# The first recurrent columns multiplied inside the modulation stage of a one-core diffusion block

## What is computed

```python
m_lat = split(silu(c) @ w_mod + b_mod, 6)            # shift, scale, gate, ... for x
m_ctx = split(silu(c_ctx) @ w_mod + b_mod, 6)        # the same for ctx
hx = rmsnorm(x, norm_mix) * (1 + m_lat[1]) + m_lat[0]
hc = rmsnorm(ctx, norm_mix) * (1 + m_ctx[1]) + m_ctx[0]
qx, kx, vx, lx, lgx, bgx, cgx, ux, gx = split_cols(hx @ w_in)   # and of hc
lru = scans(gates(conv(lx)), from ctx) * gelu(lgx)   # recurrent branch, both directions
```

## Time and profile before

| | us |
|---|---|
| median of 3 runs | 2921.41 (2920.41 to 2923.23) |
| the profiled execution, its time | 2924.9 |
| its span | 2922.7 |
| PE busy in the span | 2596.3 (89%) |
| DVE busy | 1912.2 (65%) |
| ACT busy | 947.9 (32%) |
| mean granted PE clock | 0.977 |

### The profile page before, as it was taken

How to read it: one execution, slowest core, us unless ns; L and a number is a source line. 1 busy time by engine, 2 the same in 40 slices (tenths; PEclk the granted TensorE clock), 3 DMA queues, 4 the chain that set the end, 5 groups by cost and what they waited for, 6 DMA issues and landing times.

```text
span 2922.7 us, 30747 instructions
## 1 busy us (share of the span) xinstructions
PE 2596.3 (89%) x11077; PEld 1764.0 (60%) x11077; DVE 1912.2 (65%) x2614; ACT 947.9 (32%) x1303; POOL 560.2 (19%) x580
## 2 busy tenths in 40 slices
PE   5899999999999999999999997777878877777777
PEld 3578877888777899998887843232434323332332
DVE  2589997434777778887556865666555665556656
ACT  3477875433554333333444211111101111111110
POOL 0000000000000000000000653433333333333333
PEclk7899999999999999999999999999999999999999
DMA  8733335543327788886575999999999999999998
GB/s 353 295 115 119 116 110 195 190 157 115 130 87 297 299 320 335 337 338 258 202 273 220 396 421 422 421 421 422 421 421 421 421 421 421 421 422 421 421 421 345
DMA packets 126356, 901.77 MB, mean 309 GB/s; under 512 B 14000, under 2 KB 15536, under 8 KB 17200
## 3 DMA queue, kind: packets, MB, share of 16 engines
q0 software_dynamic: 82944, 604.02, 50.1%
q1 hardware_dynamic: 38448, 276.84, 25.1%
q10 hardware_dynamic: 4864, 19.61, 1.7%
HBM read 898.29 MB, written 2.13 MB: 308 GB/s over the span
## 4 chain that ended last, share of the span: by engine, by line
PE 53%; DMA 36%; DVE 5%; issue 4%; ACT 1%; POOL 0%; POOLq 0%; ACTq 0%; DVEq 0%
DMA u<-in_peer_u,idx 31%; PE ps L473 12%; PE ps L516 8%; PE ps L518 8%; PE ps L517 8%; PE ps L488 6%; DVE u L1994 3%; DMA v<-in_peer_v,idx 2%; PE ps L870 2%; DMA w<-in_stream 2%; PE ps L582 2%; PE ps L893 1%; PE ps L699 1%; PE ps L682 1%; PE ps L531 1%
## 5 line engine op out<-in xcount | busy, mean ns | idle before, releaser
L893 PE MATMUL ps<-v,dg 128*128 128x512 f32 x1920 | 901.4, 618 | 246.2 <-DMA v<-in_peer_v,idx 205.2
L1994 DVE SCALAR_TENSOR_TENSOR u<-u,hN 128x2048 f32<-128x2048 f32 x256 | 586.5, 2291 | 461.0 <-DMA u<-in_peer_u,idx 460.8
L893 PEld LDWEIGHTS ps<-v,dg 128*128 128x128 f32 x1920 | 359.7, 195 | 782.2 <-issue 437.1
L1356 DVE TENSOR_TENSOR wl<-w,wh 128x1024 fp32r<-128x1024 f32 x428 | 519.8, 1222 | 360.4 <-ACT wh L992 359.8
L992 ACT ACTIVATE wh<-w 128x1024 fp32r<-128x1024 f32 x428 | 450.9, 1059 | 606.3 <-PE ps L518 400.2
L2100 POOL DMA_INDIRECT u<-in_peer_u,idx x256 | 260.8, 1019 | 930.9 <-DVE u L1994 546.8
L473 PE MATMUL ps<-both,wh 128*128 128x256 f32 x2048 | 371.8, 284 | 0.0
L1296 ACT ACTIVATE dg<-con,wt 128x128 f32<-128x128 f32 x240 | 92.7, 399 | 807.5 <-PE ps L893 802.5
L473 PEld LDWEIGHTS ps<-both,wh 128*128 128x128 f32 x2048 | 320.1, 192 | 3.5 <-issue 3.3
L473 PE MATMUL ps<-both,wl 128*128 128x256 f32 x1024 | 289.8, 283 | 0.0
L2084 POOL DMA_DIRECT2D mr<-in_wmod x64 | 34.0, 532 | 1306.0 <-DVE br_lo L1743 893.3
(11 more groups left out here) (287 smaller groups left out, 2737.1 us busy)
## 6 DMA issues: line engine op xcount, KB each, us to landing
w<-in_stream SPq DMA_DIRECT2D x258, 1024.0 KB, 4.9
mr<-in_wmod POOLq DMA_DIRECT2D x64, 1024.0 KB, 7.1
wg<-in_gates ACTq DMA_DIRECT2D x8, 512.0 KB, 3.4
wx<-in_stream SPq DMA_DIRECT2D x4, 1024.0 KB, 9.2
u<-in_peer_u,idx POOLq DMA_INDIRECT x256, 16.8
v<-in_peer_v,idx POOLq DMA_INDIRECT x256, 18.0
xs<-in_ctx ACTq DMA_DIRECT2D x1, 2048.0 KB, 16.4
xs<-in_x ACTq DMA_DIRECT2D x1, 2048.0 KB, 25.7
```

The costliest lines, as they stand in the source:

```text
L893: last = mm(ps[:, b, :], dg[:, k % 4, :], V[n % NV][:, b * 512:(b + 1) * 512], start=(k == 0), stop=(k == TOPK - 1))
L1356: tt(wl[p % SPLITS][:, :, :], W[s][:, q * PIECE:(q + 1) * PIECE, :], wh[p % SPLITS][:, :, :].bitcast(F32), ALU.subtract)\
L1994: stt(U[n % NU][:, :], U[n % NU][:, :], 1.0, hN[t][:, :], ALU.mult, ALU.mult, accum_out=dot[:, t, k:k + 1])\
```

## The change

- SP issues the loads of `par`, `ctx` and `x` ahead of the first halves; ACT issues only `con`. ACT waits for `par` alone, DVE for `con` before `sel`. Squares and scaling of the tokens follow at once.
- The transposes move into turn 1 of the modulation, four k-tiles behind each half (`x_turned`), over three banks (5 to 7) instead of four.
- The two halves of the first 256 columns of `lx` go to buffers `E[0]`, `E[1]` of their own (where `xs` lay), loaded among the halves after turns 2 and 3; slots 0 and 1 aren't loaded again for them.
- `early(k)`: two plain fp32 products of 128x512, weights of `E` stationary, the modulated k-tile of `xT` (both sides) moving, into banks 6 and 7. 13 of the 16 calls stand behind halves of turns 3 to 7 (`EARLY_AT`), number 13 ahead of the last `rows_turn`, 14 and 15 behind it. `first_piece` is gone, with its four splits and four lows; `hi_done` and `lo_done` are raised by four instead.
- `pads(0)` reads banks 6 and 7. Lows 4 and 5 come directly behind the last `tile_lows`, then the memset of `pad`, which waits for the last early product, then the load of `wg`, split 6, the pads and split 7.
- `mod_rows` and `mod_cols` follow the turns one by one; the exception for turn 2 is gone.

```diff
+        E = [sb(f"e{i}", R_BR + i * HB, [P, HK, CW]) for i in (0, 1)]
...
+        EARLY_AT = {(3, 0): (0,), (3, 1): (1,), (3, 2): (2,), (3, 3): (3,), (4, 0): (4,), (4, 1): (5,), (4, 3): (6,),
+                    (5, 0): (7,), (5, 3): (8,), (6, 0): (9,), (6, 3): (10,), (7, 0): (11,), (7, 3): (12,)}
+        EARLY_BANK = 6
...
+            sp.dma_start(par[:, :], a_params).then_inc(par_in, 16)
+            sp.dma_start(xs[:, 0:2, :], a_ctx.rearrange("(t p) d -> p t d", p=P)).then_inc(xc_in, 16)
+            sp.dma_start(xs[:, 2:4, :], a_x.rearrange("(t p) d -> p t d", p=P)).then_inc(xs_in, 16)
...
+                    if i == MODS and s < 2:
+                        sp.sem_inc(arrived[s], 16)
+                        continue
                     sp.dma_start(W[s][:, :, :], a_stream[i * RING + s].rearrange("p (k n) -> p k n", n=CW)).then_inc(arrived[s], 16)
+                if i in (2, 3):
+                    sp.wait_ge(*P0.at(0, f"xT{KT - 1}"))
+                    sp.dma_start(E[i - 2][:, :, :], a_stream[LRU0 + i - 2].rearrange("p (k n) -> p k n", n=CW)).then_inc(e_in[i - 2], 16)
...
-                    if n == 1 and c and c != 3:
+                    if n == 1 and c:
                         rows_turn(c - 1)
+                    if c == 1:
+                        x_turned(4 * n)
+                    for k in EARLY_AT.get((c, n), ()):
+                        early(k)
...
+            def x_turned(k0):
+
+                if k0 == 0:
                     pe.wait_ge(*A0.at(0, "xn1"))
                     pe.wait_ge(*V0_.at(0, "xn3"))
...
+                for k in range(k0, k0 + 4):
+                    if k >= 3:
+                        pe.wait_ge(xt_copied[(k - 3) % 2], (k - 3) // 2 + 1)
+                    for t in range(4):
+                        last = nc.tensor.transpose(ps[:, 5 + k % 3, t * P:(t + 1) * P], xs[:, t, k * P:(k + 1) * P], ident)
+                    last.then_inc(*P0.inc(f"xT{k}"))
+
+            def early(k):
+
+                pe.wait_ge(e_in[k // HK], 16)
+                pe.wait_ge(*VV.at(k, "x"))
+                pe.wait_ge(*AH.at(k, "vc"))
+                for blk in (0, 1):
+                    last = mm(ps[:, EARLY_BANK + blk, :], E[k // HK][:, k % HK, blk * P:(blk + 1) * P], xT[:, k, :],
+                              start=(k == 0), stop=(k == KT - 1))
+                if k == KT - 1:
+                    last.then_inc(piece_used, 4)
+
+            pe.wait_ge(*V0_.at(0, "st"))
+            for c in range(MODS):
                 mod_turn(c)
+            early(KT - 3)
             rows_turn(MODS - 1)
-            for p in range(4):
-                first_piece(p)
+            early(KT - 2)
+            early(KT - 1)
...
-            pads(0, 2 * LRU0 + 4)
+            pads(0, 2 * LRU0 + 4, EARLY_BANK)
...
             tile_lows(MODS - 2)
             tile_lows(MODS - 1)
-            low(LRU0, 0, 0, 2)
-            low(LRU0, 0, 0, 3)
+            dve.sem_inc(lo_done, SPLITS)
+            low(LRU0, 0, 0, 4)
+            low(LRU0, 0, 0, 5)
             dve.wait_ge(*VH.at(KT - 1, "lo_x"))
+            dve.wait_ge(piece_used, 2 * LRU0 + 4)
             nc.vector.memset(pad[:, :, :, :], 0.0).then_inc(*VZ.inc("lru"))
```

More of the change, by code:

```diff
@@ L296, in build @@
         apart_count = [sem("apart_dve"), sem("apart_pool")]
-        par_in, xs_in = sem("par_in"), sem("xs_in")
+        par_in, con_in, xc_in, xs_in = sem("par_in"), sem("con_in"), sem("xc_in"), sem("xs_in")
+        e_in = [sem(f"e_in{i}") for i in (0, 1)]
         wg_in, x2_in, m_in = sem("wg_in"), sem("x2_in"), sem("m_in")
@@ L945, in _ @@
             fn = nc.scalar.activation
-            act.dma_start(par[:, :], a_params).then_inc(par_in, 16)
-            act.dma_start(con[:, :], a_consts).then_inc(par_in, 16)
-            act.wait_ge(par_in, 32)
+            act.dma_start(con[:, :], a_consts).then_inc(con_in, 16)
+            act.wait_ge(par_in, 16)
             fn(sig0[:, :], pc("c", 0, 2 * KT), ACT.Sigmoid).then_inc(*A0.inc("sig"))
@@ L964, in _ @@
             fn(lm[2][:, :], lm[1][:, :], ACT.Exp, scale=-1.0).then_inc(*A0.inc("ez"))
[L965 to L968, removed]
             for i in range(4):
+                act.wait_ge((xc_in, xs_in)[i // 2], 16)
                 if i:
@@ L980, in _ @@
                 act.wait_ge(*P0.at(0, f"xT{k}"))
-                fn(xT[:, k, :], ps[:, 4 + k % 4, :], ACT.Copy).then_inc(xt_copied[1], 1)
+                fn(xT[:, k, :], ps[:, 5 + k % 3, :], ACT.Copy).then_inc(xt_copied[1], 1)
             def split(first, turn, per, p, slots=None):
@@ L989, in split, with pads @@
                     return
-                if first != LRU0 or p >= SPLITS:
+                if first != LRU0 or p >= 2 * SPLITS:
                     act.wait_ge(piece_used, turn * per + (2 * first + p - SPLITS + 1))
                 fn(wh[p % SPLITS][:, :, :], W[s][:, q * PIECE:(q + 1) * PIECE, :], ACT.Copy).then_inc(hi_done, 1)
-            for c in range(MODS - 1):
+            for c in range(MODS):
                 tiles(c)
[L997 to L1001, removed]
+            act.sem_inc(hi_done, SPLITS)
+            split(LRU0, 0, 0, AHEAD - 1)
+            split(LRU0, 0, 0, 5)
             act.wait_ge(*VZ.at(0, "lru"))
             act.dma_start(wg[:, :, :, :], a_gates[0].rearrange("p (b g n) -> p b g n", b=2, g=4)).then_inc(wg_in, 16)
-            split(LRU0, 0, 0, AHEAD - 1)
-            split(LRU0, 0, 0, 5)
             split(LRU0, 0, 0, 6)
-            def pads(j, used):
+            def pads(j, used, bank=0):
                 act.wait_ge(piece_used, used)
@@ L1013, in pads @@
                     act.wait_ge(*VT.at(j - 1, f"tap{b}3"))
-                    fn(pad[:, b, :, LRU_TAPS // 2:LRU_TAPS // 2 + T], ps[:, b, :].rearrange("p (s t) -> p s t", s=2), ACT.Copy)\
+                    fn(pad[:, b, :, LRU_TAPS // 2:LRU_TAPS // 2 + T], ps[:, bank + b, :].rearrange("p (s t) -> p s t", s=2), ACT.Copy)\
                         .then_inc(*AD.inc(f"pad{b}"))
-            pads(0, 2 * LRU0 + 4)
+            pads(0, 2 * LRU0 + 4, EARLY_BANK)
             split(LRU0, 0, 0, 7)
@@ L1346, in _ @@
             tt(sQ[:, :, 0:2], by_k(sig0[:, :]), by_k(pc("c", 0, 2 * KT)), ALU.mult).then_inc(*V0_.inc("st"))
+            dve.wait_ge(con_in, 16)
             nc.vector.reduce_sum(sel[:, :], ident.rearrange("p (g v) -> p v g", v=QUAD), AX.X).then_inc(*V0_.inc("sel"))
@@ L1416, in _ @@
             tsc(cof[:, 1, :], lm[5][:, :], -8.0, None, ALU.mult).then_inc(*V0_.inc("c8"))
-            for c in range(2):
-                mod_rows(c)
-                mod_cols(c)
             dve.wait_ge(*A0.at(0, "rt"))
@@ L1424, in _ @@
                 tsc(xs[:, i, :], xs[:, i, :], rin0[:, i:i + 1], None, ALU.mult).then_inc(*V0_.inc(f"xn{i}"))
-            mod_rows(2)
-            mod_rows(3)
+            mod_rows(0)
             for k in range(0, KT, 2):
                 dve.wait_ge(*P0.at(0, f"xT{k}"))
-                nc.vector.tensor_copy(xT[:, k, :], ps[:, 4 + k % 4, :]).then_inc(xt_copied[0], 1)
+                nc.vector.tensor_copy(xT[:, k, :], ps[:, 5 + k % 3, :]).then_inc(xt_copied[0], 1)
+                if k == 2:
+                    mod_cols(0)
             dve.wait_ge(xt_copied[1], KT // 2)
             dve.wait_ge(xt_copied[0], KT // 2)
[L1432 to L1441, removed]
+            values_x(0)
+            mod_rows(1)
+            for c in range(1, MODS - 1):
                 mod_cols(c)
@@ L1445, in _ @@
                 mod_rows(c + 1)
-            tile_lows(MODS - 2)
             mod_cols(MODS - 1)
             values_x(MODS - 1)
-            low(LRU0, 0, 0, 0)
-            low(LRU0, 0, 0, 1)
+            tile_lows(MODS - 2)
             tile_lows(MODS - 1)
-            low(LRU0, 0, 0, 2)
-            low(LRU0, 0, 0, 3)
+            dve.sem_inc(lo_done, SPLITS)
+            low(LRU0, 0, 0, 4)
+            low(LRU0, 0, 0, 5)
             dve.wait_ge(*VH.at(KT - 1, "lo_x"))
+            dve.wait_ge(piece_used, 2 * LRU0 + 4)
             nc.vector.memset(pad[:, :, :, :], 0.0).then_inc(*VZ.inc("lru"))
@@ L1556, in lru_turn @@
                 lru_out(j, 1)
-            low(LRU0, 0, 0, 4)
-            low(LRU0, 0, 0, 5)
             low(LRU0, 0, 0, 6)
@@ L1615, in _ @@
             dve.wait_ge(gains_in, 32)
-            dve.wait_ge(par_in, 32)
+            dve.wait_ge(con_in, 16)
             turned = lambda x: x.rearrange("p t (a s j) -> p t a s j", a=2, s=2)
```

## The result

| | before | after |
|---|---|---|
| median, us (6 runs each) | 2923.25 | 2903.06 |
| range | 2920.41 to 2926.05 | 2900.1 to 2905.19 |
| the profiled execution: time, span | 2924.9, 2922.7 | 2905.19, 2903.1 |
| mean granted PE clock | 0.977 | 0.988 |

The ratio is 0.9934 with a 95% interval of 0.9923 to 0.9944: 0.66% faster by the ratio, 20.2 us by the medians. Forecast was 22.5 us, from 2921.4 to 2899; the runs lie between 2900 and 2905, inside 2893 to 2910.

The account below looks back on a forecast made before the run. HBM was taken to bound the kernel until about 108 us, then PE. A clean gain of 25.4 us, less 3 us for the clock, gave 22.5 with rounding: 2921.4 to 2899 us, range 2893 to 2910.

Parts of the forecast that it names:

- What bounds, and where the gain is measured: HBM sets the pace until about 108 us, then PE without a gap; gain read at the L473 start, 135.22 us.
- Part 1: Behind the modulation: the 96 first-column products leave the path, 23.45 us, with four splits and four lows.
- Part 2: Inside the modulation: 16 calls of early(k), each two plain fp32 products, 1.72 us each, 27.5 us in all.
- Part 3: DMA stream: 40.4 MB before the last modulation half at 420 GB/s, landing at 98.6 us if never idle.
- Part 4: Turns 3 to 7: 47.3 us of PE work in 49.6 us of stream, so PE has 2.3 us to spare.
- The clock: PE at half speed: 2 us taken off for the start of turn 1, 1 us for a relapse before turn 3.
- The tail: From the last half at 98.6 us to L473 at 109.6 us, then 0.2 us lost before the gate products.
- B: Clock falls back several times in turns 3 to 7, up to 4.6 us each; 2909 us; chance 14%.
- C: Clock stays at 0.50 all through the modulation stage; 24 us slower, 2945 us; chance 4%.
- D: DVE holds back the recurrent turns, so the gain doesn't reach the end; 2919 us; chance 2%.
- E: Stream keeps its old mean of 371 GB/s because PE in turn 1 blocks buffers; gain 12.8 us, 2909 us; chance 5%.

Follow-up runs that it names:

- the order alone: Against the kernel before: only the new order of loads and transposes, first columns multiplied behind the modulation as before; 2917.32 us, ratio 0.9979.
- half the products: Changed kernel with early(k) making only its first 128 columns, the second 128 left out but for k = 0; 2896.49 us, one run.
- a filled pause: Changed kernel with 20 plain fp32 products of 128x128 into an unused bank between turns 2 and 3; 2900.72 us, one run.
- spread calls: Changed kernel with the same 13 calls spread, two in the pause behind turn 2, at most three in a turn; 2898.65 us, one run.
- the second chip: The changed kernel run again unedited on another chip; 2901.39 us, against 2923.51 for the kernel before there.
- the third: The changed kernel run again unedited on a third chip; 2902.79 us, against 2923.15 for the kernel before there.

## Why the prediction was right, point by point

- *What bounds, and where the gain is measured.* Right. The chain behind the first gate product has moved as a whole, 20.1 us at that mark, 20.0 at L722 in the attention, 19.6 at the end.
- *Part 1, 23.45 us off the path.* Right; as the run of the order alone shows, they are worth that only if the stage gives PE the time.
- *Part 2, early(k) at 1.72 us.* Mis-sized by a tenth: a call behind a half takes 1.91 us, behind turned rows 1.82, two in a row 3.63. The row of the gate products held for products that follow one another (3.44 for 8 instructions); the first one behind a narrow product costs 0.19 us more, the length of one weight load in the earlier trace rows. So the loads are hidden within a call and one per call isn't: the first load of a call begins only with the call itself (both at 62.07 us), where the first loads of the gate products begin at 126.39 and the products at 126.51. A call behind a wait pays it too (3.67 us for early(14) and (15)). 13 calls cost 2.2 us that the sum didn't have. But halves and rows behind other work took 1.00 and 0.98 us for 1.07 and 1.05, and gave back most of it: from the first half of turn 3 to the last half PE was busy 49.7 us, 46.8 without the relapse, where the sum has 46.2.
- *Part 3, last half at 98.6 us if the stream never idles.* (The loss in 65 to 75 us is 6.4 us by the rows, not 6.6; no term uses it.) It came at 103.8, 5.2 us later; the forecast had 3 us of that, as clock. First half 1.2 us late (17.39 for 16.2); half 12, the first of turn 3, at 51.5 where 13 transfers of 2.49 us from there give 49.8, 1.6 us, cause open; the rest, 2.4 us, is PE, as the kernels with half the products, with a filled pause and with spread calls show alike (101.37, 101.14, 100.88; 1.6 to 2.9 us before the three executions of the changed kernel).
- *Part 4, PE has 2.3 us to spare.* This step failed in its logic more than in its prices, which were 0.6 us off. I set PE's spare time against the last half only, and let it cover the relapse before turn 3. But the stream can run ahead of PE by four buffers and no more: when PE is late in turn 3, by four calls and a relapse, buffers stay full, the stream idles (396, 362, 387 GB/s), and what it didn't carry then isn't caught up by a PE that is early in turn 7. The trace shows both at once: the last half 2.4 us late, and PE idle 2.6 us of the 20 before it (0.59, 1.03 and 1.01 us). So the spare time has to be there when PE falls behind. Spread calls, same work, removed the loss, and so did the filled pause with four calls left in turn 3: four buffers cover the calls, but not the calls and a relapse.
- *The clock.* I took off 3 us for it, 2 at the start and 1 for the relapse. The 1 us came from half of 3 to 6 us, which no row showed, less a cover of 2.3. The relapse before turn 3 measured 2.9 us (half speed from 51.5 to 57.1 us), and came out as 2.4 us at the last half; the slow start of turn 1 cost nothing that could be shown. So the 3 us lay in partly the wrong place, and that the whole came within 2.3 us of the measured gain is in part luck. The Trainium skill ("TensorE: Matmul & The Clock Gate", section "What's actually happening") says that the array is throttled by default and activity releases it; that fits the mean clock of the whole, 0.988 for 0.977, and the pause: 4.80 us of idle, then half speed.
- *The tail.* 11.0 us forecast, 10.9 measured, and the 0.2 to 0.5 us lost before the gate products were 0.5 (12.06 us from L487 to L605 for 11.51).
- *The rivals.* B occurred once in the profiled execution, at the start of turn 3, and its price lay in the range given; on the second chip PE also worked at half speed at 46.1 us and in the tail, on the third again at 91.5 us, so B is part of the normal scatter and not excluded. C (all at half speed) didn't: the clock stood at 1.00 from 66 us on. D didn't: the marks show it. E, a stream at its old mean of 371 GB/s, didn't, though 66 to 76 us came to 362. The 358 GB/s of the Trainium skill's page "DMA: Bandwidth & Descriptors", section "Where 436 GB/s comes from", is no limit here: 424 GB/s over 10 us in the changed kernel, 418 to 423 from 56 to 96 us in the spread one.

## What to carry to other kernels

Work moved under a stream is free only as long as the engine never falls further behind than the ring's buffers cover; sum it turn by turn, with the buffers as the only credit. Here four calls in one turn were covered while the clock held, and a relapse of 2.9 us on top was not, so keep a relapse's worth in hand and put the first calls into the first pause, which takes their time out of the full turns. Two halves of an edit can be worth more together than apart (7 and 5 us, 20 together), when one makes the time that the other fills. And when calls go under a wait, look at what stands between the last transfer and the first dependent chain on other engines: one call on the wrong side of it cost 1.8 us.

## What the runs showed of the hardware

- A wide plain fp32 product behind narrow ones (32 columns stationary) costs 0.19 us more than behind its like (1.91 us for 4 instructions, 3.63 for 8, 3.44 for 8 behind wide fp32r products), and behind a wait about as much (3.67). The same trace shows 0.19 us for one load of 128 columns, and that load doesn't begin before the call.
- The granted clock of a window and the price of its instructions can differ at the start of a run: the windows of the changed kernel show 1.00 from 16 to 26 us, where its first halves take 1.93 us, as long as at 0.50. The price of an instruction was the surer sign.

```profile
16.00:26.00 10.00, 6.54 (x64) 2.29 (x64) 2.77 (x4) 8.28 (x8) 0.00 (x0) 1.00 1.01 420
```

- The place of a fall to half speed changes from execution to execution of one kernel. early(0) took 3.71, 3.49 and 2.47 us in three executions of the changed kernel, early(14) and (15) 3.67 and 5.37. Those two stand behind the same wait of 1.2 us each time, with PE at work before it but for one wait of 1.0 us; the granted clock of their stretch is 0.68 on the second chip (109.6 to 115.0 us) and 1.00 in the first execution (109.3 to 115). That moves the marks by up to 1.2 us between equal kernels, and smaller effects than that were not to be had here.
